# Attention block on one core: queries scaled straight from PSUM, a new order of exponentials, row sums and output halves

## The reference

```python
aq = rms_norm(aq.reshape(b, s, ATT_HEADS, ATT_HEAD_DIM), q_norm_gain[l])
...
scores = jnp.einsum('bcqkgd,bcskd->bckgqs', qc, kb).astype(jnp.float32) * (ATT_HEAD_DIM ** -0.5)
...
scores = jnp.where(valid[None, :, None, None, None, :], scores + bias, -jnp.inf)
sink = jnp.broadcast_to(sinks..., scores.shape[:-1] + (1,))
probs = jax.nn.softmax(jnp.concatenate([scores, sink], axis=-1), axis=-1)[..., :-1]
out = jnp.einsum('bckgqs,bcskd->bcqkgd', probs.astype(vb.dtype), vb)
...
mix = jnp.concatenate([rms_norm(att, g_attn_out[l]), rms_norm(mh, g_mlstm_out[l])], axis=-1)
x = x + mix @ w_out[l]
```

## Time and profile before

| | us |
|---|---|
| median of 3 runs | 1023.62 |
| lowest, highest | 1022.70, 1024.15 |
| the profiled execution's own time | 1022.94 |
| its span | 1021.1 |

### The profile page before, as it was taken

One profiled execution on the slowest core, in us unless ns is written; L12 is line 12 of the kernel. 1 busy time (PEld: TensorE's weight loads), 2 busy tenths in 40 slices (PEclk: granted clock), 3 DMA queues, 4 the chain that ended last, 5 costly groups with the idle time before them and its releaser, 6 DMA issues.

```text
span 1021.1 us, 13479 instructions
## 1 busy us (share of the span) xinstructions
PE 1005.1 (98%) x4970; PEld 831.3 (81%) x4970; DVE 646.9 (63%) x775; ACT 442.5 (43%) x912; POOL 691.5 (68%) x543
## 2 busy tenths in 40 slices
PE   9999999999999999999999999999999999999998
PEld 7898788877877887778888888888888888888886
DVE  4259426648862579584857676574848676574585
ACT  7555135547840558433434252433434252433440
POOL 0128768826566514988778688688778688688792
PEclk9999999999999999999999999999999999999999
DMA  7213202140131002111211211211211211211213
GB/s 228 68 53 91 77 28 67 60 154 22 32 110 57 25 18 82 52 42 42 83 42 42 83 42 42 82 42 42 83 42 42 83 42 42 83 41 43 84 58 136
DMA packets 71161, 66.06 MB, mean 65 GB/s; under 512 B 5304, under 2 KB 53688, under 8 KB 71096
## 3 DMA queue, kind: packets, MB, share of 16 engines
q1 hardware_dynamic: 70104, 64.71, 20.4%
q10 hardware_dynamic: 992, 0.49, 0.2%
HBM read 60.48 MB, written 4.21 MB: 63 GB/s over the span
## 4 chain that ended last, share of the span: by engine, by line
PE 91%; DVE 4%; issue 2%; ACT 2%; POOL 1%; DMA 0%; SPq 0%; DVEq 0%; POOLq 0%; ACTq 0%
PE banks L795 29%; PE banks L797 28%; PE banks L796 28%; PE banks L815 1%; ACT prob L1489 1%; PE banks L989 1%; PE banks L886 1%; DVE af_lo L2030 1%; PE banks L964 1%; POOL wr_raw L725 0%; PE banks L898 0%; DMA w_raw<-in_w_in 0%; PE banks L953 0%; PE banks L908 0%; PE banks L862 0%
## 5 line engine op out<-in xcount | busy, mean ns | idle before, releaser
L731 POOL TENSOR_TENSOR wr_lo<-wr_raw,wr_hi 128x512 fp32r<-128x512 f32 x231 | 318.8, 1412 | 26.8 <-ACT wr_hi L1309 21.7
L725 POOL TENSOR_TENSOR wr_raw<-wr_raw,wr_raw 128x512 f32<-128x512 f32 x132 | 193.8, 1473 | 138.0 <-PE banks L797 105.9
L795 PE MATMUL banks<-hf_hi,wr_hi 128*128 128x512 f32 x616 | 240.8, 391 | 1.8 <-DVE sg L2006 1.1
L797 PE MATMUL banks<-hf_hi,wr_lo 128*128 128x512 f32 x616 | 240.4, 390 | 0.0
L796 PE MATMUL banks<-hf_lo,wr_hi 128*128 128x512 f32 x616 | 240.1, 390 | 0.0
L1309 ACT ACTIVATE wr_hi<-wr_raw 128x512 fp32r<-128x512 f32 x231 | 136.7, 625 | 158.9 <-POOL wr_raw L725 100.4
L2109 DVE TENSOR_TENSOR x<-banks,x 128x1024 f32<-128x1024 f32 x138 | 168.8, 1224 | 53.3 <-PE banks L797 39.4
L795 PE MATMUL banks<-w_hi,actT_hi 128*128 128x512 f32 (+1 forms) x448 | 173.3, 387 | 0.9 <-DVE w_lo L1700 0.9
L797 PE MATMUL banks<-w_hi,actT_lo 128*128 128x512 f32 (+1 forms) x448 | 168.2, 376 | 0.0
L796 PE MATMUL banks<-w_lo,actT_hi 128*128 128x512 f32 (+1 forms) x448 | 167.8, 375 | 0.0
L795 PEld LDWEIGHTS banks<-hf_hi,wr_hi 128*128 128x128 f32 x616 | 115.6, 188 | 27.4 <-DVE sg L2006 2.0
(11 more groups left out here) (202 smaller groups left out, 1197.0 us busy)
## 6 DMA issues: line engine op xcount, KB each, us to landing
wr_raw<-in_w_up SPq DMA_DIRECT2D x46, 256.0 KB, 3.3
wr_raw<-in_w_gate SPq DMA_DIRECT2D x44, 256.0 KB, 3.4
wr_raw<-in_w_down SPq DMA_DIRECT2D x44, 256.0 KB, 3.1
w_raw<-in_w_in SPq DMA_DIRECT2D x32, 256.0 KB, 3.5
w_raw<-in_w_out SPq DMA_DIRECT2D x16, 256.0 KB, 2.7
x<-in_x SPq DMA_DIRECT2D x8, 512.0 KB, 6.4
out<-x SPq DMA_DIRECT2D x16, 256.0 KB, 2.1
x_in<-in_x SPq DMA_DIRECT2D x7, 512.0 KB, 4.0
```

The lines of the kernel that those rows point to most:

```text
L725: nc.gpsimd.tensor_tensor(wr_raw[slot(q, f)][:, :], wr_raw[slot(q, a)][:, :], wr_raw[slot(q, b)][:, :], ALU.subtract).then_inc(wsum, 1)
L731: nc.gpsimd.tensor_tensor(wr_lo[s][:, :], wr_raw[s][:, :], wr_hi[s][:, :].bitcast(F32), ALU.subtract).then_inc(wf_lo, 1)
L795: nc.tensor.matmul(ps, x_hi, wh, start=first, stop=False, skip_group_check=more)
L797: return nc.tensor.matmul(ps, x_lo, wh, start=False, stop=last, skip_group_check=more)
```

## The change

- **Queries.** ScalarE only squares the accumulator; the copy aq and its two buffers go. VectorE multiplies the inverse root by `rstd` (qscale, 128x8) and makes qn from the accumulator in PSUM. The accumulator is therefore free when qn is done: query units from 34 on wait for qn of two units before, and the two halves of the first output unit wait for qn of tiles 6 and 7.
- **Order on ScalarE.** Unit 32's Square stands ahead of the last state squares of the mLSTM; the inverse root stands in front of the squares of the attention's output; the Square ahead of the rounding of mh.
- **Order on VectorE.** qss of tile 0 stands ahead of the last mLSTM tile's outputs, later ones ahead of the bias additions. actT_lo of mh stands behind qn. The sinks are negated once, the maximum comes out negated, and esk is made after ScalarE has its signal for the exponentials. In output units of the first eight, the copy of pT, dsum and the scaling of probabilities stand between half a's addition and half b's (function `probabilities`).
- **Row sums.** They are made in bank 7, behind the values of the pass, and copied behind the bias additions. The mh transposes no longer wait for that copy, the probability transposes do.

The core of the diff (left out: the new semaphores, the tiles nsink in smx's place and qscale, and from VectorE's loop the block that now is `probabilities`):

```diff
@@ -222,13 +223,11 @@
-        aq0, e = place("aq0", [P, N], at=e)
-        aq1, e = place("aq1", [P, N], at=e)
-        qT, prob, pT, aqs = [qT0, qT1], [prob0, prob1], [pT0, pT1], [aq0, aq1]
+        qT, prob, pT = [qT0, qT1], [prob0, prob1], [pT0, pT1]
@@ -822,7 +825,9 @@
                 ps = bank[U % 2][:, 0:width]
-                if U >= 2:
+                if U >= 4 * T + 2:
+                    pe.wait_ge(qn_ready, U - 4 * T - 1)
+                elif U >= 2:
                     pe.wait_ge(acc_free[U % 2], U // 2)
@@ -914,8 +919,8 @@
                     pe.wait_ge(ssa_ready, t)
-                pe.wait_ge(mixb_ready, min(t + 4, T))
-                nc.tensor.matmul(bank[3][:, 0:1], sqb[:, 0:P], ones[:, 0:1], start=True,
+                pe.wait_ge(pTd, min(t + 2, T))
+                nc.tensor.matmul(bank[7][:, 0:1], sqb[:, 0:P], ones[:, 0:1], start=True,
                                  stop=True).then_inc(ssa_mm, 1)
@@ -930,8 +935,6 @@
                     pe.wait_ge(mixb_ready, t)
-                if t >= 4:
-                    pe.wait_ge(ssa_ready, t - 3)
                 for kk in range(4):
@@ -956,6 +959,8 @@
             def att_prob_transposes(t):
+                if t >= 2:
+                    pe.wait_ge(ssa_ready, t - 1)
                 for kv in range(KV):
@@ -1001,7 +1006,7 @@
                     if j == 0:
-                        pe.wait_ge(acc_free[part], UNITS // 2)
+                        pe.wait_ge(qn_ready, T - 1 + part)
                     else:
@@ -1085,14 +1090,14 @@
                     pe.wait_ge(mh_ready, T)
-                if 0 <= s - 5 < T:
-                    att_sumsq(s - 5)
                 if 0 <= s - 1 < T:
...
                     att_values(s - 4)
+                if 0 <= s - 5 < T:
+                    att_sumsq(s - 5)
                 s = U - 6 * T
@@ -1371,16 +1376,18 @@
                 else:
-                    if t == 0:
-
-                        act.wait_ge(num_done, T)
                     if t >= 1:
                         act.wait_ge(q_stat, t)
-
-                    step(nc.scalar.activation(pq[:, :], ps[:, :], ACT.Square, scale=r_))
-                    if t >= 2:
-                        act.wait_ge(qn_ready, t - 1)
-                    nc.scalar.activation(aqs[t % 2][:, :], ps[:, :], ACT.Copy, scale=r_).then_inc(free, 1)
+                    nc.scalar.activation(pq[:, :], ps[:, :], ACT.Square, scale=r_).then_inc(pq_ready, 1)
+
+            def state_squares(t):
+
+                act.wait_ge(mh_ready, t + 1)
+                if t == 0:
+                    act.wait_ge(it_exp, 1)
+                nc.scalar.activation(msq[:, :], mh[:, t, :], ACT.Square,
+                                     accum_out=ss2[:, t, 1:2]).then_inc(ssb_done, 1)
+                act.wait_ge(ssb_done, t + 1)
             for U in range(ALL):
@@ -1432,13 +1439,8 @@
                     last.then_inc(it_exp, 1)
-                if 1 <= s <= T:
-                    act.wait_ge(mh_ready, s)
-                    if s == 1:
-                        act.wait_ge(it_exp, s)
-                    nc.scalar.activation(msq[:, :], mh[:, s - 1, :], ACT.Square,
-                                         accum_out=ss2[:, s - 1, 1:2]).then_inc(ssb_done, 1)
-                    act.wait_ge(ssb_done, s)
+                if 1 <= s < T:
+                    state_squares(s - 1)
                 s = U - 4 * T
@@ -1455,12 +1457,21 @@
                                          ACT.Copy, scale=cols[:, G_Q:G_Q + 1]).then_inc(qT_ready, 1)
+                if 0 <= s < T:
+                    evacuate(U)
+                if s == 0:
+                    state_squares(T - 1)
+                if 0 <= s - 1 < T:
+                    tt = s - 1
                     act.wait_ge(mh_tp, tt + 1)
...
                 if 0 <= s < T:
-                    evacuate(U)
+                    act.wait_ge(q_stat, s + 1)
+                    if s >= 1:
+                        act.wait_ge(q_scale, s)
+                    inverse_root(qrs[:, :], qss[:, :], HD).then_inc(q_rs, 1)
                 if 0 <= s - 4 < T:
@@ -1470,11 +1481,6 @@
                                          ACT.Copy).then_inc(mixa_hi, 1)
-                if 0 <= s < T:
-                    act.wait_ge(q_stat, s + 1)
-                    if s >= 1:
-                        act.wait_ge(qn_ready, s)
-                    inverse_root(qrs[:, :], qss[:, :], HD).then_inc(q_rs, 1)
                 if 0 <= s - 6 < T:
@@ -1488,6 +1494,7 @@
                                                   accum_out=dsum[:, j:j + 1]))
+                    act.wait_ge(sink_shift, tt + 1)
                     nc.scalar.activation(esk[:, :], esk[:, :], ACT.Exp).then_inc(p_exp, 1)
@@ -1726,6 +1733,33 @@
                 ins.then_inc(conv_ready, 1)
+            def query_stats(t):
+
+                dve.wait_ge(pq_ready, t + 1)
+                if t >= 1:
+                    dve.wait_ge(q_rs, t)
+                V_.tensor_reduce(qss[:, :], pq[:, :].rearrange("p (h d) -> p h d", h=HEADS), AX.X,
+                                 ALU.add).then_inc(q_stat, 1)
+
+            def probabilities(s):
+
+                if 0 <= s - 4 < T:
+                    tt = s - 4
+                    dve.wait_ge(pt_done, tt + 1)
+                    if tt >= 2:
+                        dve.wait_ge(pv_done, tt - 1)
+                    V_.tensor_copy(pT[tt % 2][:, 4:8, :],
+                                   bank[7][:, :].rearrange("p (k n) -> p k n", k=4)).then_inc(pTd, 1)
+                if 0 <= s - 3 < T:
+                    tt = s - 3
+                    dve.wait_ge(p_exp, tt + 1)
+                    link(V_.tensor_tensor(dsum[:, :], dsum[:, :], esk[:, :], ALU.add))
+                    V_.reciprocal(dsum[:, :], dsum[:, :]).then_inc(p_inv, 1)
+
+                    dve.wait_ge(p_inv, tt + 1)
+                    V_.tensor_tensor(prob[tt % 2][:, 4:8, :], prob[tt % 2][:, 4:8, :], bcast(dsum[:, 4:8], P),
+                                     ALU.mult).then_inc(p_ready[1], 1)
+
             kview = kvs[:, :, 2 * MH:2 * MH + KV * HD]
@@ -1752,6 +1786,7 @@
                                             heads.unsqueeze(2).to_broadcast([CHUNK, KV, 2, 2])))
+                    V_.tensor_scalar(nsink[:, :], sink_b[:, :], -1.0, None, ALU.mult).then_inc(nsink_ready, 1)
                 if U == T + 1:
@@ -1843,6 +1878,8 @@
                     V_.memset(den4[:, :], 0.0).then_inc(gates_done, 1)
+                if U == 4 * T:
+                    query_stats(0)
                 s = U - 3 * T
@@ -1904,6 +1941,8 @@
                                             ALU.add).then_inc(wa_free, 1)
+                    if j < T:
+                        probabilities(U - 4 * T)
                     if j >= T + 6:
@@ -1914,34 +1953,10 @@
                 s = U - 4 * T
-                if 0 <= s - 5 < T:
-                    tt = s - 5
-                    dve.wait_ge(ssa_mm, tt + 1)
-                    V_.tensor_copy(ss2[:, tt, 0:1], bank[3][:, 0:1]).then_inc(ssa_ready, 1)
...
-                if 0 <= s - 1 < T:
-                    tt = s - 1
-                    dve.wait_ge(mixb_hi, tt + 1)
-                    a = slice(tt % 4 * P, (tt % 4 + 1) * P)
-                    V_.tensor_tensor(actT_lo[:, tt // 4, 4:8, a],
-                                     bank[3][:, :].rearrange("p (k n) -> p k n", k=4),
-                                     actT_hi[:, tt // 4, 4:8, a].bitcast(F32),
-                                     ALU.subtract).then_inc(mixb_ready, 1)
+                if U < UNITS:
+                    probabilities(s)
+                if 1 <= s < T:
+                    query_stats(s)
                 if 0 <= s - 2 < T:
@@ -1960,29 +1975,37 @@
                     steps[0] += 1
-                if 0 <= s < T:
-
-                    dve.wait_ge(acc_free[U % 2], U // 2 + 1)
-                    if s >= 1:
-                        dve.wait_ge(q_rs, s)
-                    V_.tensor_reduce(qss[:, :], pq[:, :].rearrange("p (h d) -> p h d", h=HEADS), AX.X,
-                                     ALU.add).then_inc(q_stat, 1)
+                if 0 <= s - 5 < T:
+                    dve.wait_ge(ssa_mm, s - 4)
+                    V_.tensor_copy(ss2[:, s - 5, 0:1], bank[7][:, 0:1]).then_inc(ssa_ready, 1)
                 if 0 <= s - 2 < T:
...
                     dve.wait_ge(s_evac, tt + 1)
-                    link(V_.tensor_reduce(smx[:, :], prob[tt % 2][:, :, :], AX.X, ALU.max))
-                    link(V_.tensor_tensor(smx[:, :], smx[:, :], sink_b[:, :], ALU.max))
-                    link(V_.tensor_scalar(nmx[:, :], smx[:, :], -1.0, None, ALU.mult))
-                    V_.tensor_tensor(esk[:, :], sink_b[:, :], nmx[:, :], ALU.add).then_inc(s_max, 1)
+                    if tt == 0:
+                        dve.wait_ge(nsink_ready, 1)
+                    link(V_.tensor_reduce(nmx[:, :], prob[tt % 2][:, :, :], AX.X, ALU.max, negate=True))
+                    V_.tensor_tensor(nmx[:, :], nmx[:, :], nsink[:, :], ALU.min).then_inc(s_max, 1)
```

(16 more changed lines are left out.)

22 lines of the change are left out of this document (6 added, 16 removed).

## The result

| | before | after |
|---|---|---|
| median (runs of one comparison) | 1023.88 (4) | 1012.64 (4) |
| lowest, highest | 1022.70, 1025.51 | 1012.32, 1012.90 |
| profiled execution, span | 1022.94, 1021.1 | 1012.72, 1010.9 |

The ratio is 0.9889, with an interval of 0.9872 to 0.9906: faster by 1.1%. Forecast were 1016.4 us and a range of 1015.2 to 1019.6. Between the profiled executions the gain is 10.2, where 7.2 were forecast. One run of the kernel before in a later comparison (1113 us, at a mean clock of 0.85) fell in a slower state and is left out of every comparison.

The account below looks back on a forecast made before the run. TensorE, busy 98%, was taken as the bound, with only its pauses winnable. Terms 1.67 + 1.2 + 0.6 + 0.5 + 1.65 + 1.65 - 0.1 = 7.2; 1023.62 - 7.2 = 1016.4 us, range 1015.2 to 1019.6.

Parts of the forecast that it names:

- The ceiling: Six TensorE pauses between 207 and 316 us, about 7.65 us together; outside its pauses nothing could be won.
- W1: First query transposes wait for qn of tile 0, listed 1.51 us; earlier squares and no aq remove it whole, -1.67.
- W2: Values of tile 0 wait 1.54 us for copy qT of tile 3; earlier exponentials shrink it to 0.4, -1.2.
- W3: The mh transposes of tile 7 wait 0.46 us for the row-sum copy ss; moving the sums removes it, -0.6.
- W4: Values of tile 5 wait about 0.4 us for VectorE's half of pT; copying pT before half b's addition gives -0.5.
- W5: Values of tile 6 wait 1.51 us for ScalarE's half of pT; earlier bias additions and exponentials give -1.65.
- W6: Values of tile 7 wait 1.51 us for VectorE's half of pT; copying pT before half b's addition gives -1.65.
- The additions of 0.15 for modelled ends: At TensorE's six pauses: true pauses 0.07 to 0.16 us longer each than listed, since a matmul's end is modelled.
- Half b's wait for qn of tile 7: First output unit's second half: the one new wait, costing +0.1 us, bounds 0 and 1.3.
- qn from PSUM, charged at nothing: VectorE's qn in the query units: reading PSUM instead of SBUF was charged no extra time.
- The ring through the row sums: Rival, 3%, slower: values, row sums, ss, exponentials and pT close a ring, costing from 9.8 us a pass on.
- the failing margins: Rival, 22%: a margin of 0.1 to 0.4 us fails, losing 1 to 4 us of gain; 1017.4 to 1020.4.

Follow-up runs that it names:

- before_pad32: The kernel before with an unused tile of 32 bytes a partition behind qrs, no instruction changed; median 1019.19 us.
- after_aq_late: The kernel after with ScalarE's copy aq back, its buffers behind pT1 so that unit 32's Square needs no wait for the mLSTM's numerators; 1012.20 us.

## Why the prediction was right and wrong

The step that failed is the sentence behind the sum: "What comes behind hangs on TensorE ... so all of it should reach the end." All of it did reach the end, but the part behind the stage was charged at nothing, as if its matmuls had one pace in both kernels. All of the stage's gain was forecast, 7.2 against 7.08. The term that was missing is 2.6 us of the feed-forward: qscale, which I priced as an instruction of 0.2, was also a tile of 32 bytes, and moved everything behind it to a multiple of 128. The slow pace stood in the trace of the kernel before (0.2325 a matmul for down products with slot 1, 0.2267 for most others), but I read the feed-forward only for its waits. A busy time of 98% hid it.

The ceiling fell with it. "Outside its pauses nothing can be won" was wrong: a thousandth of a microsecond on each of 2436 matmuls, 2.5 us, was more than any of the six waits.

Of the gain of 11.2 between the medians the stage is 7.1 and the pace 2.6. The last 1.5 is 0.3 before the stage, 0.3 at the very end, and 1 us by which the kernel before's median stands above its profile. I had set that at 0.68 and taken it for the same in both; the kernel after has none, and why is open.

Point by point in the stage:

- **W1, forecast -1.67, measured -1.69.** The Square stood at 205.59 (forecast 205.9), qss at 206.31 (206.6), qn at 211.54 (forecast 211.8), the transposes without a wait:

```profile
205.59 0.69 ACT L1381 ACTIVATE pq<-banks,rstd 128x512 f32<-128x512 f32 x1 [3.19 <-PE banks L800]
...
209.94 0.63 ACT L1388 ACTIVATE msq<-mh 128x512 f32<-128x512 f32 x1 [3.66 <-DVE mh L1899]
```

```profile
207.53 1.00 DVE L1895 TENSOR_TENSOR den<-den,enm 128x4 f32<-128x4 f32 x1
...
211.27 0.23 DVE L1994 TENSOR_SCALAR qscale<-qrs,rstd 128x8 f32<-128x8 f32 x1 [1.36 <-ACT qrs L1265]
211.54 0.69 DVE L1997 TENSOR_TENSOR qn<-banks,qscale 128x512 f32<-128x512 f32 x1
```

  What I did not see: 0.87 of W1 was the held instruction on den. In before_pad32 it took 0.16, and W1 was 0.6 there with the old order (the instruction before, then in before_pad32):

```profile
207.79 1.03 DVE L1858 TENSOR_TENSOR den<-den,enm 128x4 f32<-128x4 f32 x1
```

```profile
207.48 0.16 DVE L1859 TENSOR_TENSOR den<-den,enm 128x4 f32<-128x4 f32 x1
```

  That is half of this term, and it changes by execution: that the forecast met it so closely is partly luck.
- **W2, -1.2 against -1.24.** Exponentials of tile 1 at 233.12 (forecast 233.4). The held min is there, and so is the rest of the wait, 0.3:

```profile
231.86 1.22 DVE L1987 TENSOR_TENSOR nmx<-nmx,nsink 128x8 f32<-128x8 f32 x1
```

```profile
237.60 0.66 PE L994 MATMUL banks<-pT,v_prev 128*64 128x128 f32 x8 [0.30 <-ACT qT L1458]
```

- **W3, -0.6 against -0.61.**
- **W4, W5, W6: -0.5, -1.65, -1.65 against -0.39, -1.49, -1.50.** The mechanism was right: with the old order alone all three came back. The additions of 0.15 for modelled ends were too much here: the starts agree with the waits as listed.
- **Half b's wait for qn of tile 7, +0.1 against 0.** qn ended at 271.36, half b began at 271.62. The margin is a quarter of a microsecond.

```profile
270.67 0.69 DVE L1997 TENSOR_TENSOR qn<-banks,qscale 128x512 f32<-128x512 f32 x1
```

- **qn from PSUM, charged at nothing: right.** 0.69 as from SBUF; after_aq_late, which reads SBUF, is not faster from unit 33 on. The Trainium skill (VectorE: DVE Perf Modes, section on the TRN2 errata) gives a PSUM source more fixed cycles than an SBUF source, by estimate 65 ns; the rows do not show them. The Trainium skill also says (GPSIMD Engine Reference, Specifications) that GpSimd shares its SBUF interfaces with VectorE instructions of two SBUF inputs. The traces agree: qn took 0.95 or 0.96 in four of its eight tiles before, tile 7's among them, and 0.69 in all eight now.
- **The rivals.** The ring through the row sums and the failing margins did not occur.

The range was too narrow because it was built from the terms of the stage alone. It had no case for a cost that the change moves without touching an instruction.

## What to carry to other kernels

Compare the start of the same matmul along the whole run, not only waits and busy shares: a slope between two flat parts is a change of pace, and needs another cause than a step. When a diff adds or removes a tile, look at which tiles move and by how much; here 32 bytes were worth a third of what a reordering of three engines was worth. Before a wait is judged by its length, look at the clock behind it, in more than one execution and in the mean clock of every run, and at tiny instructions in front of it that are held in some executions and not in others.
